# The first group's up products computed whole, and plain small operands written out directly, in a one-core encoder layer

## The chip, the cores and the metric

The kernel runs on one core of one Trainium2 chip. The metric is the device time of one execution in microseconds (us), as the median of several. The profile shows one execution, taken by the hardware profiler, with its own time.

The core's engines each have a queue of their own: TensorE (PE; its weight loads are listed as PEld), VectorE (DVE), ScalarE (ACT), GpSimd (POOL) and SyncE (SP), which here only issues DMA transfers. In the profile, "SPq" and "ACTq" are the DMA issues of SP's and ACT's instruction streams.

## What is computed

One encoder layer over 1280 tokens (256 and 1024), width 1024, in float32, and a final norm:

```python
def swiglu(h, w_gate, w_up, w_down):
    return (jax.nn.silu(h @ w_gate) * (h @ w_up)) @ w_down

for l in range(DEPTH):                      # DEPTH = 1, D_MODEL = 1024, D_FF = 2816
    x = x + 0.5 * swiglu(rmsnorm(x, norm_ffn1[l]), w_ffn1_gate[l], w_ffn1_up[l], w_ffn1_down[l])
    x = x + hybrid_mixer(rmsnorm(x, norm_mix[l]), w_in[l], ...)
    x = x + 0.5 * swiglu(rmsnorm(x, norm_ffn2[l]), w_ffn2_gate[l], w_ffn2_up[l], w_ffn2_down[l])
return rmsnorm(x, norm_final)
```

The change lies in the gate and up products of the two feed-forward blocks, called FFN1 (f = 0) and FFN2 (f = 1) here. `hybrid_mixer` (attention and gated linear attention) is not touched, but for the counts of some semaphores that it shares.

## The kernel before

Every float32 product is made in three passes with a high and a low part of each operand (`w_hi`, `w_lo`; hi x hi, hi x lo, lo x hi). The tokens are split in two halves of 640 (`HTOK`, five pairs of 128-token tiles), the 1024 inputs in two halves of 512, and the 2816 columns of a weight go in 11 groups of 256, two halves of 128. So a group of gate or up is a product of 2 x 2 blocks, and it is made by one level of Strassen's method in Winograd's form: seven products, GP1 to GP7, whose moving operand (640 columns) is a plain or combined block of the normed activations and whose stationary operand is a plain or combined block of the weight. The index q counts gate and up groups alternately, 0 to 21: q even is gate, q odd is up, and the two share the group number i = q // 2.

**Turns.** A product is made in two turns, c = 0 and 1, since 640 columns don't fit one PSUM bank. A turn has 384 or 256 columns and 12 matmuls; from q = 1 on the 256-column turn is "wide": 4 matmuls of 512 columns (two passes at once) alternate with 4 of 256. Which turn is wide depends on f. The table `GORDER` lists all turns in PE's order. The step number s counts products; `GORDER` begins with the c = 0 turns of the first `G_FIRST` = 4 steps, since the last token pair (columns of c = 1) is normed last.

**The second level.** The product GP2 (A12 times B21, B21 being activations) enters only output block C11. So the GP2 of gate and that of up of one group are joined and made by a second level: seven inner products of 320 columns (L1 in two turns, LA, LB, LB, LC, LC), each 6 matmuls, placed among the turns of the up entry (q odd). Their moving operands are seven "pieces" of B21: three plain quarters (m = 0, 1, 6) and four sums T1 to T4 (m = 2 to 5), each as high and low part, 640 KB. Group 0 uses a piece while it is made in one of two SBUF buffers; ACT's queue stores each piece into the DRAM tensor `inner_mid` (`L1630`, seven stores of 640 KB per FFN), and the groups from 1 on load them back through SP's queue into three buffers `in_b` (`L971`). For the inner weight sums, ACT keeps A12 of gate in `in_a` (`L1581`).

**Who does what around the first group.** `norm_blocks` (ACT from `L1537`, DVE from `L2092`) cuts a turned token pair from PSUM into the plain operands (GP1, GP3, B21) and the sums t1 to t4; B21 is kept in float32 only (`hs_f`). PE turns a pair with `norm_turn` (matmuls against `ident`, `L2791`), and begins the next pair only when DVE has done the low parts of an earlier one (`N["lo"]`, 6 per pair). Per weight block, ACT casts the high part (`L1574`) and DVE makes the low part (`L2132`) and the sums (`L2207` to `L2217`), five steps ahead of PE (`G_RING`). DVE adds each product from PSUM to the sums `first_p`, `first_u` (P1, U2, U3; `second_p`, `second_u` in FFN2) at `L2257`; ACT copies GP1 out of its bank (`L1592`), takes silu of finished gate blocks (`L1605`); POOL multiplies finished up blocks in. Products share PSUM banks, two for each kind of turn: GP1 (and GP2, where it is whole) uses the Z banks, GP6, GP7 and GP4 the X banks, GP5 and GP3 the Y banks. PE may write a Z bank again only when ACT's copy of GP1 is done (`kept`). Each engine runs its instructions in program order, and a DMA issue stands in the stream of the engine that issues it.

Of the kernel before, what the change touches and what calls it, by code (L numbers as in the profile page):

```python
# [30 lines left out]
P = 128  # L31
# [64 lines left out]
NP = 7  # L96
# [7 lines left out]
GU_FIRST = (GP1, GP6, GP5, GP7, GP4, GP3)  # L104
# [21 lines left out]
G_OUT = (GP7, GP4, GP3)  # L126
G_PAIRS = 2 * GROUPS
G_ENTRIES = [(q, j) for q in range(G_PAIRS) for j in (GU_UP if q % 2 else GU_GATE if q else GU_FIRST)]
# [6 lines left out]
def entry(q, j):  # L135
# [26 lines left out]
PIECE_AT = {(0, GP5, 1): 0, (0, GP7, 1): 1}  # L162
PIECE_AT.update(((1, *e), m + 2) for m, e in enumerate(INNER[:N_INNER - 2]))
PIECE_SUMS_AT = {(0, GP5, 1): 1, (0, GP4, 1): 2, (1, GP6, 1): 3, (1, GP5, 1): 4}


def a12_kept(s):

    q, j = G_ENTRIES[s]
    return q % 2 == 0 and j == (GP6 if q else GP3)  # L170


def inner_marks():

    act, dve, pool = [], [], [("b_lo", 0), ("b_lo", 1)]
    for s, c in GORDER:
        q, j = G_ENTRIES[s]
        i = q // 2
        if j == GP1 and q == 0:
            act += [("cg", 0, c)]  # L180
        if j == GP7 and c == 1 and q and q % 2 == 0:
            act += [("cg", i, 1)]
# [79 lines left out]
def build(nc, x_prompt, x_sample, norm_ffn1, w_ffn1_gate, w_ffn1_up, w_ffn1_down, norm_mix, w_in, attn_sink,  # L262
# [4 lines left out]
    with ctx:  # L267
# [60 lines left out]
        second = inner_places(1, 17920, 165888, (77312, 159744, 164864), 171520, 82432)  # L328
# [19 lines left out]
        first = inner_places(0, 161792, 133120, (122880, 128000, 133120), 138240, 140800)  # L348
# [388 lines left out]
        def cg_kept(f, i, c):  # L737
            return inner_act(f, "cg", i, 1 if i else c)
# [2564 lines left out]
```

## Time and profile before

| | |
|---|---|
| device time, median of three executions | 2182.32 us (2181.51 to 2184.72) |
| the profiled execution, its own time | 2181.47 us |
| span of its trace | 2179.3 us |
| PE busy | 2133.5 us, 98% of the span |
| DVE busy | 1613.6 us, 74% |
| ACT busy | 878.8 us, 40% |
| POOL busy | 381.5 us, 18% |
| DMA, mean over the span | 185 GB/s |

The trace covers 2179.3 us of the execution's 2181.47 us; the other 2.17 us lie around it. A row of the timeline gives the start, the duration, the engine, the source line, the operation, what is written and read, and the shape; behind it, in brackets, how long the engine had been idle and what released it. Matmuls overlap, so what one costs is the distance from its start to the next one's. "x2" at the end means two instructions in one row.

### The profile page before, as it was taken

To read this page: it belongs to the slowest core of one execution; us is meant where nothing else is said; L and a number is where in the kernel's file an instruction comes from. 1 tells how busy PE (TensorE), PEld (TensorE's weight loads), DVE (VectorE), ACT (ScalarE), POOL (GpSimd) and SP (SyncE) were. 2 spreads that over 40 slices of the span, in tenths; PEclk is the share of its full clock that TensorE was granted. 3 is DMA by queue.
4 is the path that set the end of the run, shared out by engine and by line. 5 is a ranking of instruction groups with operands and counts; after the bars stand their busy time and mean duration, and the time that the engine had idled before them with its cause. 6 is when DMAs were issued, how large, how long until landed. Compare 5 with 4: busy or idle time off the path is not lost.

```text
span 2179.3 us, 33661 instructions
## 1 busy us (share of the span) xinstructions
PE 2133.5 (98%) x11992; PEld 1919.0 (88%) x11992; DVE 1613.6 (74%) x2928; ACT 878.8 (40%) x1731; POOL 381.5 (18%) x363
## 2 busy tenths in 40 slices
PE   6899999999999999999999999899999999999998
PEld 5899999999988888888888888789999999988887
DVE  7877887888666686988754556778888788857676
ACT  7333333332343355855553334433333333343343
POOL 7311111211100002201012335321211111200000
PEclk9999999999999999999999999999999999999999
DMA  3555566556696566433255972255565556687554
GB/s 127 202 185 166 178 195 202 195 189 196 221 304 210 174 206 167 129 105 102 87 150 171 302 226 95 96 199 194 190 198 183 166 181 200 214 290 255 176 189 165
DMA packets 268168, 402.15 MB, mean 185 GB/s; under 512 B 26658, under 2 KB 162210, under 8 KB 268004
## 3 DMA queue, kind: packets, MB, share of 16 engines
q1 hardware_dynamic: 257348, 377.72, 53.9%
q10 hardware_dynamic: 10656, 22.29, 2.7%
q8 instruction: 97, 1.59, 0.3%
q14 instruction: 67, 0.55, 0.1%
HBM read 298.04 MB, written 97.65 MB: 182 GB/s over the span
## 4 chain that ended last, share of the span: by engine, by line
PE 92%; DVE 4%; issue 1%; ACT 1%; DMA 1%; SPq 0%; ACTq 0%; POOL 0%; POOLq 0%; DVEq 0%
PE ps L2863 14%; PE ps L2859 10%; PE ps L2861 8%; PE ps L2862 8%; PE ps L2871 8%; PE ps L2872 8%; PE ps L2873 8%; PE ps L2760 3%; PE ps L2762 3%; PE ps L2761 3%; PE ps L2815 2%; PE ps L2817 2%; PE ps L2816 2%; PE ps L2778 2%; PE ps L2780 2%; PE ps L2779 2%
## 5 line engine op out<-in xcount | busy, mean ns | idle before, releaser
L2871 PE MATMUL ps<-w_hi,dh 128*128 128x512 f32 x770 | 300.2, 390 | 0.0
L2873 PE MATMUL ps<-w_hi,dh 128*128 128x512 f32 x770 | 299.7, 389 | 0.0
L2863 PE MATMUL ps<-hs,w_lo 128*128 128x384 f32 (+1 forms) x848 | 261.7, 309 | 0.0
L2305 DVE TENSOR_TENSOR dh<-dr,dh 128x640 fp32r<-128x640 f32 x154 | 128.7, 835 | 158.9 <-ACT dh L1651 158.7
L2872 PE MATMUL ps<-w_lo,dh 128*128 128x512 f32 x620 | 241.2, 389 | 0.0
L1651 ACT CAST dh<-dr 128x640 fp32r<-128x640 f32 x154 | 111.9, 727 | 260.6 <-PE ps L2873 234.0
L1574 ACT CAST w_hi<-w_raw 128x512 fp32r<-128x512 f32 x154 | 95.1, 620 | 259.1 <-PE ps L2817 181.9
L2861 PE MATMUL ps<-hs,w_hi 128*128 128x384 f32 (+1 forms) x552 | 185.0, 335 | 2.8 <-DVE hs L2097 2.8
L2862 PE MATMUL ps<-hs,w_hi 128*128 128x384 f32 (+1 forms) x552 | 185.0, 335 | 0.0
L2859 PE MATMUL ps<-hs_first,w_hi 128*128 128x512 f32 x504 | 182.7, 396 | 0.0
L2859 PE MATMUL ps<-hs,w_hi 128*128 128x512 f32 x504 | 180.2, 391 | 0.0
L2862 PE MATMUL ps<-hq,w_hi 128*128 128x384 f32 x528 | 177.3, 336 | 0.0
L2873 PEld LDWEIGHTS ps<-w_hi,dh 128*128 128x128 f32 x770 | 144.5, 188 | 30.3
L2871 PEld LDWEIGHTS ps<-w_hi,dh 128*128 128x128 f32 x770 | 144.6, 188 | 30.0
L2863 PEld LDWEIGHTS ps<-hs,w_lo 128*128 128x128 f32 x848 | 160.2, 189 | 0.0
L2760 PE MATMUL ps<-h_hi,w_hi 128*128 128x512 f32 (+1 forms) x432 | 156.9, 363 | 0.0
L2762 PE MATMUL ps<-h_hi,w_lo 128*128 128x512 f32 (+1 forms) x432 | 153.3, 355 | 0.0
L2761 PE MATMUL ps<-h_lo,w_hi 128*128 128x512 f32 (+1 forms) x432 | 153.2, 355 | 0.0
L2861 PE MATMUL ps<-hq,w_hi 128*128 128x384 f32 x440 | 148.3, 337 | 4.6 <-DVE second_u L2257 3.5
L2872 PEld LDWEIGHTS ps<-w_lo,dh 128*128 128x128 f32 x620 | 116.4, 188 | 23.8
L2132 DVE TENSOR_TENSOR w_lo<-w_sum,w_hi 128x512 fp32r<-128x512 f32 x106 | 84.7, 799 | 67.8 <-ACT w_hi L1574 67.6
L1574 ACT CAST w_hi<-w_sum 128x512 fp32r<-128x512 f32 x132 | 81.1, 615 | 131.9 <-DVE w_sum L2217 74.3
(363 smaller groups left out, 5372.3 us busy)
## 6 DMA issues: line engine op xcount, KB each, us to landing
in_b<-inner_mid SPq DMA_DIRECT2D x140, 640.0 KB, 5.2
dr<-hid_mid SPq DMA_DIRECT2D x154, 320.0 KB, 3.5
w_raw<-in_w_ffn_down SPq DMA_DIRECT2D x176, 256.0 KB, 3.8
hid_mid<-st SPq DMA_DIRECT2D x88, 320.0 KB, 5.1
w_raw<-in_w_ffn_gate SPq DMA_DIRECT2D x44, 512.0 KB, 5.2
w_raw<-in_w_ffn_up SPq DMA_DIRECT2D x44, 512.0 KB, 5.0
hid_mid<-sg SPq DMA_DIRECT2D x66, 320.0 KB, 3.8
inner_mid<-piece ACTq DMA_DIRECT2D x14, 640.0 KB, 4.1
```

The costliest lines, as they stand in the source:

```text
L1574: nc.scalar.copy(g_block(s)[0][:, 0:k, :], src).then_inc(B["hi"], 1)
L2305: v.tensor_tensor(a_lo, DR[f][n % D_HID][:, :], a_hi.bitcast(F32), ALU.subtract).then_inc(W["a_lo"], 1)
L2760: mm(out, hi, rhs_hi, start=first, stop=False)
L2761: mm(out, hi, rhs_lo, start=False, stop=False)
L2762: return mm(out, lo, rhs_hi, start=False, stop=last)
L2859: mm(ps[:, G_BANKS[j][c], :], hi[:, k, :], h_both(f, j, c, k), start=begins, stop=False, skip_group_check=True)
L2861: mm(out, hi[:, k, :], b_hi, start=begins, stop=False, skip_group_check=True)
L2862: mm(out, hi[:, k, :], b_lo, start=False, stop=False, skip_group_check=True)
L2863: last = mm(out, lo[:, k, :], b_hi, start=False, stop=k == 3, skip_group_check=True)
L2871: mm(out, hi, w_h, start=first and p in D_FRESH, stop=False, skip_group_check=True)
L2872: mm(out, hi, w_l, start=False, stop=False, skip_group_check=True)
L2873: return mm(out, lo, w_h, start=False, stop=last, skip_group_check=True)
```

## The change

- **The first group is made whole** (`WHOLE = 2`): q = 0 and 1 use the seven products of one level, GP2 among them, and no inner product. The inner products begin with group 1 (q = 3). For GP2 of q = 0, silu reads the PSUM bank and writes C11's place; for q = 1, DVE multiplies GP2 in (`g_mult`). In these two entries U3 is begun by GP7 and ended by GP5. `GORDER` now begins with the c = 0 turns of five steps.
- **`norm_blocks`** writes the high part of GP2's operand into `hs` and adds one low part per pair: 7 counts per pair where there were 6.
- **Plain pieces** (m = 0, 1, 6) are now quarters of that operand, high and low part. `whole_stores` writes them from `hs` (FFN1) or `hs_first` and `hq` (FFN2) to `inner_mid`, from ACT's queue, after turn (q = 0, GP4, c = 1): 12 DMAs of 128x5x64 float32 in FFN1, 12 of 128x2x64 and 12 of 128x3x64 in FFN2; a contiguous run on the SBUF side is 64 elements, 256 bytes.
- **The sums** T1 and T3 are made by DVE with three operations each (one part each in FFN1, two in FFN2), T2 and T4 by POOL from T1 and T2 with two each; each has one ACT cast, one POOL low part and one store of 640 KB on ACT's queue.
- **Gone**: the two ACT copies of GP1 into C11's place for q = 0, the inner products, inner weight blocks and DVE additions of group 0. The load of up's second weight half no longer waits for ACT's copy of A12 in the first group, and the sums over the first group's hidden blocks move to turns of q = 2 and wait for the store of T3.

The core of the diff:

```diff
-GU_FIRST = (GP1, GP6, GP5, GP7, GP4, GP3)
+GU_FIRST = (GP1, GP6, GP2, GP7, GP5, GP4, GP3)
-G_ENTRIES = [(q, j) for q in range(G_PAIRS) for j in (GU_UP if q % 2 else GU_GATE if q else GU_FIRST)]
+G_ENTRIES = [(q, j) for q in range(G_PAIRS) for j in (GU_FIRST if q < WHOLE else GU_UP if q % 2 else GU_GATE)]
-GORDER = ([(s, 0) for s in range(G_FIRST)] + [(s, 1) for s in range(G_FIRST)]
+GORDER = ([(s, 0) for s in range(G_LEAD)] + [(s, 1) for s in range(G_LEAD)]
...
+PIECE_AT = {(0, GP3, 1): T1, (1, GP6, 0): T2, (1, GP7, 1): T4, (1, GP3, 0): T3}
+STORES_AT = {(1, GP6, 1): T1, (1, GP5, 0): T2, (1, GP5, 1): T4, (2, GP1, 0): T3}
+WHOLE_STORES_AT = (0, GP4, 1)
...
             def norm_blocks(f, i):
-                    act.wait_ge(N["lo"], 6 * i)
+                    act.wait_ge(N["lo"], 7 * i)
-                nc.scalar.copy(b21_piece(f, pair), ps[:, b + 1, :]).then_inc(N["hi"], 1)
+                nc.scalar.copy(h_piece(f, GP2, 0, pair), ps[:, b + 1, :]).then_inc(N["hi"], 1)
...
                     nc.scalar.copy(P1[f][:, lo:hi], ps[:, Z_BANKS[c], 0:n]).then_inc(S["kept"], 1)
-                    if q == 0:
-                        nc.scalar.copy(hid(f, 0)[:, lo:hi], ps[:, Z_BANKS[c], 0:n]).then_inc(L["act"], 1)
...
+            def whole_stores(f):
+                act.wait_ge(NFF[f]["lo"], 7 * HT)
+                for m, k, half in ((0, 0, 0), (1, 1, 0), (6, 1, 1)):
+                    to = inner_mid[f, m].rearrange("p (e k t n) -> p e k t n", e=2, k=2, t=HT)
+                    for a, b in B21_PARTS[f]:
+                        for e in range(2):
+                            for x in range(2):
+                                act.dma_start(to[:, e, x, a:b, :], b21(f, e, k, half, a, b)[:, x, :, :]
+                                             ).then_inc(b21_stored, 16)
...
                 if 1 in parts:
                     dve.wait_ge(N["hi"], 8 * i + 4)
+                    lo(GP2, b + 1)
                     t_free(3)
...
+            def g_mult(f, s, c):
+                if j == GP2 and q:
+                    v.tensor_tensor(to, to, by, ALU.mult).then_inc(L["dve"], 1)
...
+                if j == GP2:
+                    pe.wait_ge(*bank_kept(f, q, c))
```

Where it moves instructions, at three places. First ACT's stream from the end of q = 0's silu (`sg`) on. Before:

```order
L1605 ACTIVATE sg<-first_p 128x384 [waits gateup_added]
L1605 ACTIVATE sg<-first_p 128x256 [waits gateup_added]
L1574 CAST w_hi<-w_sum 128x512 [waits block_summed,gateup_done]
L1630 DMA inner_mid<-piece_0 128x1280 [waits pool_marks]
L1605 ACTIVATE sg<-first_u 128x384 [waits gateup_added]
L1605 ACTIVATE sg<-first_u 128x256 [waits gateup_added]
L1574 CAST w_hi<-in_a 128x256 [waits inner_dve,gateup_done]
L1630 DMA inner_mid<-piece_1 128x1280 [waits pool_marks]
L1592 COPY first_p<-ps 128x384 [waits gateup_silu,gateup_done]
L1592 COPY first_p<-ps 128x256 [waits gateup_silu,gateup_done]
```

The same place of the changed kernel:

```order
L1656 ACTIVATE sg<-first_p 128x384 [waits gateup_added]
L1656 ACTIVATE sg<-first_p 128x256 [waits gateup_added]
L1616 CAST w_hi<-w_raw 128x512 [waits block_summed,gateup_done]
L1679 DMA inner_mid<-hs 128x5x64 [waits norm_ffn1_lo]
L1679 DMA inner_mid<-hs 128x5x64 x11
L1656 ACTIVATE sg<-first_u 128x384 [waits gateup_added]
L1656 ACTIVATE sg<-first_u 128x256 [waits gateup_added]
L1616 CAST w_hi<-w_sum 128x512 [waits block_summed,gateup_done]
L1665 CAST piece_0<-piece_sum_0 128x640 [waits inner_dve]
L1637 COPY first_p<-ps 128x384 [waits gateup_silu,gateup_done]
L1637 COPY first_p<-ps 128x256 [waits gateup_silu,gateup_done]
```

Two stores of pieces have given way to twelve in a row, ahead of the copies (`COPY first_p<-ps`) of GP1 of q = 1. In FFN2, 24 stand there.

Second, PE's stream in q = 1, where the first turn behind GP1's wide turn stood. Before, an inner product, bound to its piece:

```order
L2859 MATMUL ps<-hs,w_hi 128x512 [waits inner_act,gateup_kept,block_lo]
L2863 MATMUL ps<-hs,w_lo 128x256
...
L2815 MATMUL ps<-piece_0,w_hi 128x320 [waits pool_marks,block_lo]
L2816 MATMUL ps<-piece_0,w_hi 128x320
L2817 MATMUL ps<-piece_0,w_lo 128x320
```

In the changed kernel, the end of GP6's wide turn and the two turns of GP2 of q = 1:

```order
L2936 MATMUL ps<-hs,w_hi 128x512
L2940 MATMUL ps<-hs,w_lo 128x256
L2938 MATMUL ps<-hs,w_hi 128x384 [waits gateup_kept,block_lo]
L2939 MATMUL ps<-hs,w_hi 128x384
L2940 MATMUL ps<-hs,w_hi 128x384
...
L2936 MATMUL ps<-hs,w_hi 128x512 [waits gateup_wide,block_lo]
L2940 MATMUL ps<-hs,w_hi 128x256
```

The turn that follows GP6 is now GP2, and it waits for `gateup_kept`, ACT's copy of GP1 of the same q.

Third, DVE's stream in FFN1's norm of the third pair. Before:

```order
L2110 TENSOR_TENSOR first_t<-first_t,ps 128x512 [waits norm_ffn1_hi,norm_ffn1_t_lo]
L2097 TENSOR_TENSOR hs<-ps,hs 128x512
L2115 TENSOR_TENSOR first_t<-ps,first_t 128x512 [waits norm_ffn1_lo,norm_ffn1_hi,norm_ffn1_t_lo]
L2120 TENSOR_TENSOR first_t<-ps,first_t 128x512 [waits norm_ffn1_lo,norm_ffn1_t_lo,norm_ffn1_hi]
L2123 TENSOR_TENSOR first_t<-ps,first_t 128x512 [waits norm_ffn1_t_lo]
L2097 TENSOR_TENSOR hs<-ps,hs 128x512
```

The changed kernel:

```order
L2157 TENSOR_TENSOR first_t<-first_t,ps 128x512 [waits norm_ffn1_hi,norm_ffn1_t_lo]
L2144 TENSOR_TENSOR hs<-ps,hs 128x512
L2162 TENSOR_TENSOR first_t<-ps,first_t 128x512 [waits norm_ffn1_lo,norm_ffn1_hi,norm_ffn1_t_lo]
L2144 TENSOR_TENSOR hs<-ps,hs 128x512 [waits norm_ffn1_hi]
L2168 TENSOR_TENSOR first_t<-ps,first_t 128x512 [waits norm_ffn1_lo,norm_ffn1_t_lo]
L2171 TENSOR_TENSOR first_t<-ps,first_t 128x512 [waits norm_ffn1_t_lo]
L2144 TENSOR_TENSOR hs<-ps,hs 128x512
```

One more low part (GP2's) has come between the sums.

## Rows read from the trace of the kernel before

**Rows 1.** Timeline of PE in FFN1: the prologue's wait, two stalls, q = 2's first matmul.

```profile
43.04 1.09 PE L2791 MATMUL ps<-ident,hs_f 128*128 128x128 f32 x8 [1.50 <-DVE first_t L2120]
...
72.75 0.61 PE L2815 MATMUL ps<-piece,w_hi 128*128 128x320 f32 x1 [2.61 <-DVE up_c L2187]
...
92.80 0.38 PE L2815 MATMUL ps<-piece,w_hi 128*128 128x320 f32 x1 [3.16 <-issue]
...
98.77 0.34 PE L2861 MATMUL ps<-hs,w_hi 128*128 128x384 f32 x1
```

**Rows 2.** Timeline of PE in FFN2: four stalls, and q = 2's first matmul.

```profile
1387.90 0.66 PE L2861 MATMUL ps<-hq,w_hi 128*128 128x384 f32 x1 [3.49 <-DVE second_u L2257]
...
1404.71 0.38 PE L2815 MATMUL ps<-piece,w_hi 128*128 128x320 f32 x1 [0.52 <-DVE up_c L2187]
...
1411.33 0.39 PE L2815 MATMUL ps<-piece,w_hi 128*128 128x320 f32 x1 [1.14 <-POOL piece L1398]
...
1424.82 0.60 PE L2815 MATMUL ps<-piece,w_hi 128*128 128x320 f32 x1 [3.64 <-issue]
...
1430.61 0.39 PE L2859 MATMUL ps<-hs_first,w_hi 128*128 128x512 f32 x1
```

**Rows 3.** Windows: stretch, length, busy (count) per engine, PEclk, DMA share, GB/s.

```profile
72.70:76.10 3.40, 3.35 (x12) 3.38 (x13) 3.07 (x7) 0.62 (x1) 0.00 (x0) 0.50 0.00 0
...
93.00:96.50 3.50, 3.50 (x14) 3.50 (x14) 2.56 (x4) 1.36 (x2) 3.24 (x3) 0.53 0.78 259
...
1387.90:1393.60 5.70, 5.70 (x21) 5.70 (x22) 2.19 (x4) 2.95 (x7) 2.08 (x2) 0.50 0.01 3
...
1424.80:1427.80 3.00, 2.98 (x10) 2.81 (x11) 1.72 (x4) 1.35 (x2) 2.40 (x3) 0.50 0.62 203
```

**Rows 4.** Timeline of PE: the spacing of matmuls of 320, 512+256 and 384 columns.

```profile
89.18 0.31 PE L2816 MATMUL ps<-piece,w_hi 128*128 128x320 f32 x1
89.33 0.31 PE L2817 MATMUL ps<-piece,w_hi 128*128 128x320 f32 x1
...
98.31 0.28 PE L2863 MATMUL ps<-hs,w_lo 128*128 128x256 f32 x1
...
98.66 0.28 PE L2863 MATMUL ps<-hs,w_lo 128*128 128x256 f32 x1
...
98.95 0.33 PE L2862 MATMUL ps<-hs,w_hi 128*128 128x384 f32 x1
```

**Rows 5.** Timeline of ACT (ACTq: DMA issues in its stream) at FFN1's first piece store.

```profile
62.55 0.53 ACT L1605 ACTIVATE sg<-first_p 128x384 f32<-128x384 f32 x1 [1.20 <-DVE first_p L2257]
62.97 0.34 ACTq L1630 DMA_DIRECT2D inner_mid<-piece  x1
62.98 0.40 ACT L1605 ACTIVATE sg<-first_p 128x256 f32<-128x256 f32 x1
63.28 0.60 ACT L1574 CAST w_hi<-w_sum 128x512 fp32r<-128x512 f32 x1
...
66.89 0.74 ACT L1592 COPY first_p<-ps 128x384 f32<-128x384 f32 x2
68.32 0.62 ACT L1574 CAST w_hi<-in_a 128x512 fp32r<-128x512 f32 x1 [0.70 <-DVE in_a L2146]
68.85 0.72 ACT L1622 CAST piece<-piece_sum 128x640 fp32r<-128x640 f32 x1
```

**Rows 6.** Timeline of SP's DMA issues: loads of `hq` in a row, one weight load.

```profile
1241.49 8.20 SPq L1198 DMA_DIRECT2D hq<-o_mid  x8
...
1266.69 10.13 SPq L1270 DMA_DIRECT2D hq<-o_mid  x20
...
1381.08 0.58 SPq L867 DMA_DIRECT2D w_raw<-in_w_ffn_gate  x1
```

**Rows 7.** Timeline of DVE: an operation beside POOL, and FFN2's wait for weights.

```profile
28.96 1.77 DVE L2213 TENSOR_TENSOR w_raw<-w_raw 128x512 f32<-128x512 f32 x1
...
1384.46 0.69 DVE L2207 TENSOR_TENSOR w_sum<-w_raw 128x512 f32<-128x512 f32 x1 [2.21 <-DMA w_raw<-in_w_ffn_up]
```

More of the change, by code:

```diff
@@ L125, with u3_first, u3_last, outputs @@
 G_ADDS = (GP6, GP5, GP7, GP4, GP3)
-G_OUT = (GP7, GP4, GP3)
+WHOLE = 2
 G_PAIRS = 2 * GROUPS
-G_ENTRIES = [(q, j) for q in range(G_PAIRS) for j in (GU_UP if q % 2 else GU_GATE if q else GU_FIRST)]
+def u3_first(q):
+    return GP7 if q < WHOLE else GP5
+def u3_last(q):
+    return GP5 if q < WHOLE else GP7
+def outputs(q):
+    return (GP2, GP5, GP4, GP3) if q < WHOLE else (GP7, GP4, GP3)
+G_ENTRIES = [(q, j) for q in range(G_PAIRS) for j in (GU_FIRST if q < WHOLE else GU_UP if q % 2 else GU_GATE)]
 G_STEPS = len(G_ENTRIES)
@@ L189, in inner_marks @@
             pool += [("mult", i)]
-        for n in [5] if s == 1 and c else G_AFTER[(s, c)] if s >= G_LEAD - 1 else []:
+        if q == 1 and j == GP2:
+            dve += [("mult", 0, c)]
+        for n in G_AFTER[(s, c)]:
             at, kind_of = G_ENTRIES[n]
-            if kind_of == GP3 and at % 2 == 0:
+            if first_difference(n):
                 dve += [("summed", at // 2, 1)]
@@ L1413, in gate_up @@
             def gate_up(f):
-                for m in range(2):
-                    piece_lo(f, m)
+                piece_sum(f, T2)
+                piece_lo(f, T1)
+                piece_sum(f, T4)
+                piece_lo(f, T2)
+                piece_lo(f, T4)
                 for s, c in GORDER:
@@ L1556, in g_hi @@
                 q, j = G_ENTRIES[s]
-                raws = [g_raw(f, q, e) for e in range(2)]
                 if s >= G_RING:
@@ L1576, in keep_a12 @@
             def keep_a12(f, i):
-                if i:
+                if i > 1:
                     act.wait_ge(*lo_made(f, 2 * i - 1, LC))
+                else:
+                    for read in b21_read(f):
+                        act.wait_ge(*read)
                 act.wait_ge(*g_loaded(f, 2 * i, 0))
@@ L1600, in g_evict @@
                     nc.scalar.copy(hid(f, 0), P1[f][:, :]).then_inc(L["act"], 1)
-                if j in G_OUT and q % 2 == 0:
-                    act.wait_ge(*added(f, s, c))
-                    src = {GP7: U3, GP4: P1, GP3: U2}[j][f][:, lo:hi]
-                    out = hid(f, {GP4: 1, GP3: 2, GP7: 3}[j])[:, lo:hi]
+                if j in outputs(q) and q % 2 == 0:
+                    if j == GP2:
+                        act.wait_ge(*done(f, s, c))
+                        src = ps[:, Z_BANKS[c], 0:n]
+                    else:
+                        act.wait_ge(*added(f, s, c))
+                        src = {u3_last(q): U3, GP4: P1, GP3: U2}[j][f][:, lo:hi]
+                    out = hid(f, {GP2: 0, GP4: 1, GP3: 2, u3_last(q): 3}[j])[:, lo:hi]
                     nc.scalar.activation(out, src, ACT.Silu).then_inc(S["silu"], 1)
@@ L2209, in g_sums @@
                     v.tensor_tensor(s2, s1, a11, ALU.subtract).then_inc(B["summed"], 1)
-                if j == GP6 and (q or f == 0):
+                if j == (GP2 if q < WHOLE else GP6) and (q or f == 0):
                     dve.wait_ge(*lo_made(f, q, GP1))
@@ L2233, in g_evict @@
                 of, rest = ps[:, G_BANKS[j][c], 0:n], ps[:, G_BANKS[j][c], 512 - n:512]
-                if two and j == GP1:
-                    to = p1[:, part]
+                if two and j in (GP1, GP2):
+                    to = (p1 if j == GP1 else u3)[:, part]
                     dve.wait_ge(*kept(f, s, c))
@@ L2736, in _ @@
             norm_blocks(1, HT - 1)
-            for s in range(2, G_FIRST):
+            for s in range(2, G_LEAD):
                 g_evict(1, s, 0)
@@ L2827, in g_step @@
                 if q == 0:
-                    name, n, count = {GP1: (NFF[f]["lo"], 6, 2), GP6: (t_low[f], 4, 2), GP7: (t_low[f], 4, 4),
-                                      GP5: (t_low[f], 4, 1), GP4: (t_low[f], 4, 3), GP3: (NFF[f]["lo"], 6, 6)}[j]
+                    name, n, count = {GP1: (NFF[f]["lo"], 7, 2), GP6: (t_low[f], 4, 2), GP2: (NFF[f]["lo"], 7, 4),
+                                      GP7: (t_low[f], 4, 4), GP5: (t_low[f], 4, 1), GP4: (t_low[f], 4, 3),
+                                      GP3: (NFF[f]["lo"], 7, 7)}[j]
                     if f and c and n == 4:
```

349 lines of the change are left out of this document (191 added, 158 removed).

## The prediction

> **What bounds the kernel now.** I read the share of busy time first: PE works 98% of the span, so a change can only take PE's work, its few waits, or the slow clock behind a wait. Then the waits of PE, and in the timeline where they lie. Around the first group of FFN1 PE stands still twice, 2.61 us before an inner product that waits for a DVE addition, and 3.16 us before the last one but one; the trace names nothing for the latter ("issue"), and in the program it waits for a piece that goes through ACT and POOL [rows 1]. In FFN2 there are four, of 3.49, 0.52, 1.14 and 3.64 us [rows 2]. Then the windows: behind four of these stalls the granted clock is 0.50 to 0.53, that is 1.2 GHz in place of 2.4, for 3.4, 3.5, 5.7 and 3.0 us [rows 3]. Half of each stretch is lost: 1.7, 1.7, 2.85 and 1.5 us. I count up to the start of q = 2, at 98.77 and 1430.61 [rows 1, 2], and take the rest of the kernel as unchanged: from there on both have the same products, and the reloaded pieces are first needed in q = 3, some 20 us later.
>
> **PE's work.** Matmuls of 384 columns are 0.17 to 0.18 us apart (98.77 to 98.95), a pair of 512 and 256 columns 0.35 (98.31 to 98.66), those of 320 columns 0.145 (89.18 to 89.33) [rows 1, 4]. So a turn of 384 columns takes 2.09, one of 256 1.40, a whole product 3.5, an inner one 0.87. Each FFN adds two products (7.0) and drops seven inner ones (6.1): **+0.9 us** each.
>
> **Stalls that go.** All six stood at inner products of group 0 or behind piece work on DVE. FFN1: 2.61 + 3.16 + 1.7 + 1.7 = **-9.2**. FFN2: 3.49 + 0.52 + 1.14 + 3.64 + 2.85 + 1.5 = **-13.1**.
>
> **The norm.** The extra low part (0.6 us of DVE per pair, by the step from one DVE row to the next, 0.69 long) delays the turning of the next pair. In FFN1 it lies on the path twice, in the first product's start and in the fourth turning, about 1.4 with the waits. But PE now does GP2's c = 0 turn before the last pair is turned, where it idled 1.50 [rows 1]; that wait goes: **-0.1** in sum. FFN2 has more cover, **-0.3**. The bounds: at best the whole 1.5 is won, at worst all five low parts lie on the path, 3.0 per FFN.
>
> **A wait that stays in FFN2.** GP4's c = 1 turn needs U3's addition, which DVE does behind its wait for up's weights (2.21 idle at 1384.46 [rows 7]). PE comes 3.2 later (GP2, less 0.3); the load is issued some 1.2 later, behind one more low part (0.6), and the two piece sums ahead of the addition (0.8) are gone: 3.49 - 3.2 + 1.2 + 0.6 - 0.8 = **+1.3**. Between 0 and the old 3.49.
>
> **The stores on ACT's queue.** This is the new thing and decides. They stand ahead of silu (two), a weight cast, a piece cast and the copy that frees GP1's bank; PE's turn of GP2 of q = 1 waits for that copy. What an issue costs, from the nearest rows: one alone 0.34, and ACT's computing runs on beside it (62.97 against 62.98, with the next operation on time) [rows 5]; so they start when the cast ahead starts, but a row of them is a chain of issues. Twenty `hq` loads of 256 runs took 10.13, 0.51 each; eight others 8.20, 1.03 each, while earlier transfers were pending; a weight load of 1024 runs behind another 0.58 [rows 6], 0.62 with the gap. I take 0.51 for FFN2's (256 and 384 runs), 0.56 for FFN1's (640 runs, between). DMA is idle at that time (share 0.00 at 72.7, 0.01 at 1387.9 [rows 3]), which is why I stay near the unburdened row.
>
> FFN1: silu of GP4's first turn, at 62.55 before [rows 5], comes one product less 0.1 later, 66.0; the cast 0.7 later at 66.7. Twelve issues: 6.7, until 73.4. Then silu 0.43 and 0.30, cast 0.53, piece cast 0.72, copy 0.37 [rows 5], 2.3 in all: 75.7. PE without stalls would begin q = 2 at 98.77 - 9.2 + 0.9 - 0.1 = 90.4, and GP2 of q = 1 five products (17.4) earlier, at 73.0. So it stands for 2.7 us, and the clock falls as it did after 2.61 (1.7). Net: -8.4 + 2.7 + 1.7 = **-4.0**.
>
> FFN2: GP4's second turn is ready at 1387.90 - 3.49 + 3.2 = 1387.6, starts at 1388.9, ends 1391.0; addition, silu, and the cast starts at 1392.2. 24 issues: 12.2, until 1404.4. The same five operations, the copy of 256 columns for 384, 2.2, and since the first turn is the wide one here, a DVE addition of 0.4: 1407.0. PE without this stall: 1430.61 - 13.1 + 0.9 - 0.3 + 1.3 = 1419.4, GP2 at 1402.0. So 5.0 of standing and, between the 1.5 and the 2.85 of before, 2.2 for the clock. Net: -11.2 + 7.2 = **-4.0**.
>
> The other new work has cover: the sums on POOL (four passes of 640 columns, then low parts) and the stores of T1 to T4 are due in q = 3, PE's 20 us. The two ACT copies that go are no path.
>
> A page bears on this. The Trainium skill, "DMA: Bandwidth & Descriptors", Specifications, gives 512 bytes as the least run at line rate and says that below it the engine reads, modifies and writes. The runs here are 256 bytes in SBUF. The rows show loads of 512-byte runs only, so no row here bears it out; by it the third case below would be the likely one.
>
> **Sum.** 2181.47 - 4.0 - 4.0 = **2173.5 us** for an execution like the profiled one, which lies 0.9 below the median of 2182.32. 0.1 us per issue is 3.6 us in all. Break-even (2181.47) is at 0.22 us more per issue, some 0.75.
>
> **Rivals.**
> 1. Cheaper stores. If an issue in a row costs as one alone, 0.38 with the gap, FFN1 gains 12 x 0.18 = 2.2 and FFN2 24 x 0.13 = 3.1: 2168.2. If ACT isn't held at all, the full 8.4 + 11.2 come: 2161.9. For it: the store beside ACT's work at 62.97 [rows 5]. Against: each `hq` issue is paced at 0.51 with SP doing nothing else [rows 6].
> 2. Nothing gained: DVE late. One DVE operation of 512 columns beside POOL took 1.77 in place of 0.69 [rows 7]. About eight of DVE's operations stand between the landing of up's weights and the cast ahead of the stores, and POOL now has four additions more there. If four of the eight in each FFN are stretched by 1.1, the stores begin 4.4 later and both gains are eaten: 2173.5 + 8.8 = 2182.3. The Trainium skill, "SBUF — State Buffer", section "SBUF: two separate sides", says of the port pair that DVE and GpSimd share that a GpSimd operation and a DVE one with two SBUF inputs exclude each other for a whole instruction; by that rule the stretch is one POOL operation long. Against it: POOL's sums begin only after T1, that is after GP3's additions, and at 62 to 70 POOL has little else.
> 3. Slower: the stores back up. At 1.03 each, as the eight `hq` loads [rows 6], FFN1 loses 12 x 0.47 = 5.6 and FFN2 24 x 0.52 = 12.5: 2191.6. It is slower by 0.2% from about 0.9 per issue. For it: short runs, twelve and 24 transfers with nothing between; against it: idle DMA engines.
>
> **How the numbers follow.** 0.2% (4.4 us) is what a measurement can tell from no change. Forecast 0.43 (2170 to 2178, of it 0.03 above 2177.1); rival 1 0.17; rival 2 0.22 (2178 to 2187, of it 0.02 beyond 2185.9); rival 3 0.18. Faster 0.40 + 0.17 = 0.57; same 0.03 + 0.20 = 0.23; slower 0.02 + 0.18 = 0.20. The range leaves out the lower half of rival 1 and the upper half of rival 3: 2165 to 2189.
>
> **What would show it.** In ACT's stream, a row of 12 issues of some 6.7 us from about 67 on, and one of 24 of some 12 us from 1392; right behind, two silus and two casts, the copy, and PE's wait at the first matmul of GP2 of q = 1, of about 2.7 and 5 us, with a half-clock stretch behind each. q = 2 starts near 94.8 and 1422.6 (1426.6 less FFN1's 4.0). No wait at an inner product of q = 3. The forecast is wrong if ACT computes on during the row, if an issue takes 0.9 or more, if the cast ahead of the row starts later than 69, or if PE waits elsewhere, above all in the norm for low parts beyond 1.5 us.

## The result: slower by 0.67%, and the profile after

The changed kernel takes 2196.77 us (median of four, 2196.49 to 2197.64), the kernel before 2182.46 us (2181.51 to 2184.72): a ratio of 1.0067, with a 95% interval of 1.0054 to 1.0079. The forecast was a gain of 8 us, to 2173.5; what came is a loss of 14.3, outside the range. The profiled execution of the changed kernel took 2196.83 us, with a span of 2195.0 beside 2179.3 before.

Its page, first the span and PE's row of section 1 (busy us, share, instructions), then the first rows of the chain that ended last:

```profile
span 2195.0 us, 33664 instructions
...
PE 2133.8 (97%) x11996; PEld 1918.8 (87%) x11996; DVE 1616.3 (74%) x2922; ACT 869.7 (40%) x1716; POOL 383.4 (17%) x364
...
PE 89%; DVE 4%; DMA 2%; issue 2%; ACT 1%; ACTq 1%; SPq 1%; POOL 0%; DVEq 0%; POOLq 0%
```

PE has nearly the same work (busy for 2133.8 us beside 2133.5, four matmuls more), so the loss is waiting and the slow clock behind a wait. The waits of PE, us in total, times, longest:

```profile
PE ps L2936 <- DVE second_u L2318: 9.2, 3, 8.5
...
PE ps L2938 <- DVE first_u L2318: 8.0, 2, 7.4
PE ps L2936 <- DVE second_p L2296: 7.7, 1, 7.7
PE ps L2938 <- ACT first_p L1637: 6.3, 2, 6.1
```

Of the six stalls of [rows 1, 2] five are gone, and of the 3.49 us one 1.00 is left (at 1394.77). Four larger ones have come, two per FFN. PE's timeline shows where:

```profile
77.35 0.66 PE L2938 MATMUL ps<-hs,w_hi 128*128 128x384 f32 x1 [6.12 <-ACT first_p L1637]
...
96.83 0.34 PE L2938 MATMUL ps<-hs,w_hi 128*128 128x384 f32 x1
...
118.28 0.66 PE L2938 MATMUL ps<-hs,w_hi 128*128 128x384 f32 x1 [7.42 <-DVE first_u L2318]
...
1415.28 0.77 PE L2936 MATMUL ps<-hs_first,w_hi 128*128 128x512 f32 x1 [7.71 <-DVE second_p L2296]
...
1434.63 0.39 PE L2936 MATMUL ps<-hs_first,w_hi 128*128 128x512 f32 x1
...
1457.15 0.76 PE L2936 MATMUL ps<-hs_first,w_hi 128*128 128x512 f32 x1 [8.49 <-DVE second_u L2318]
```

The stalls at 77.35 and 1415.28 stand before GP2 of q = 1, where the forecast put them. Those at 118.28 and 1457.15 stand at GP3 of q = 2, the last gate product but one of group 1, and no case of the forecast had them. Behind each the clock is at its lower level for some 4 us, as in [rows 3] (columns as there; 0.54 to 0.56 is a mean, with some tenths of a us at the upper level):

```profile
77.30:81.90 4.60, 4.55 (x15) 4.54 (x16) 3.48 (x7) 1.84 (x4) 1.16 (x1) 0.55 0.55 175
118.20:122.90 4.70, 4.62 (x15) 4.58 (x16) 4.63 (x9) 1.16 (x2) 0.00 (x0) 0.55 0.55 210
```

**The account by stage.** q = 2 of FFN1 starts at 96.83 in place of 98.77: 1.9 gained. FFN2's first product starts 7.0 later than before (1369.18 and 1362.14): 9.0 lost in between, 7.42 of standing and some 2 of clock. FFN2's q = 2 starts at 1434.63 in place of 1430.61, 4.0 later: 3.0 gained in FFN2's first group. The end is 15.7 later: 11.7 lost behind it, 8.49 and 2 of clock among them. So both first groups are faster, 4.9 in all, and 20.7 are lost behind them. Nearly all of that is lost at once: the 120 matmuls from q = 2's first on take 20.8 us in the trace before, and 30.4 (FFN1) and 31.1 (FFN2) now, which is 19.9 of the 20.7.

**The first kind of stall: the row of stores.** ACT's timeline in FFN1 (as [rows 5]) and the end of the row in FFN2:

```profile
66.10 8.72 ACTq L1679 DMA_DIRECT2D inner_mid<-hs  x11
74.87 0.83 ACT L1656 ACTIVATE sg<-first_u 128x384 f32<-128x384 f32 x2 [8.27 <-issue]
...
76.74 0.74 ACT L1637 COPY first_p<-ps 128x384 f32<-128x384 f32 x2
...
1412.44 0.83 ACT L1656 ACTIVATE sg<-second_u 128x256 f32<-128x256 f32 x2 [12.12 <-issue]
```

ACT stands for 8.27 and 12.12 us behind the issues. One issue takes 0.80 us in FFN1 (8.72 and a gap over 11; the first, at 65.68, took 0.42) and 0.54 in FFN2 (24 from 1399.38 to 1412.40). Then two silus, two casts and the copy, in the order forecast; PE's turn of GP2 begins with the copy's end, in FFN2 with DVE's addition behind the copy. Ahead of FFN1's row, from 60.5 to 66.0, the DMA share is 0.00; during the row the stores, with one load of weights (512 KB) beside them, keep the DMA engines busy all the time, at only 231 GB/s (columns as above, the last two DMA share and GB/s):

```profile
66.10:74.80 8.70, 5.13 (x30) 4.53 (x28) 4.48 (x7) 0.50 (x1) 3.06 (x2) 0.99 1.00 231
```

In FFN2's row the share is 0.77, at 177 GB/s.

**The second kind: a late weight load.** DVE's timeline before the stall at 118.28, and SP's issues:

```profile
115.51 0.69 DVE L2266 TENSOR_TENSOR w_sum<-w_raw 128x512 f32<-128x512 f32 x1 [7.60 <-DMA w_raw<-in_w_ffn_up]
```

```profile
100.75 1.34 SPq L999 DMA_DIRECT2D in_b<-inner_mid  x3
102.14 1.96 SPq L893 DMA_DIRECT2D hid_mid<-sg  x3
104.22 0.41 SPq L890 DMA_DIRECT2D w_raw<-in_w_ffn_up  x1
```

The kernel before, SP's issues at the same place of the program:

```profile
92.72 1.30 SPq L971 DMA_DIRECT2D in_b<-inner_mid  x3
94.07 7.32 SPq L870 DMA_DIRECT2D hid_mid<-sg  x3
101.50 0.45 SPq L867 DMA_DIRECT2D w_raw<-in_w_ffn_up  x1
```

Before, three pieces (3 x 640 KB) were issued 6 us ahead of q = 2's start and 8.8 us ahead of the weights. Now they are issued 4 us behind q = 2's start, and the weights 3.5 us behind them. They wait for DVE's last addition of T3, since the buffers `in_b` lie on the memory that T3 is made from; it ran from 99.79 to 100.6. The stores of hidden blocks stand behind the pieces in SP's stream and are held with them. So 2.9 MB (pieces and hidden blocks) stand ahead of the 512 KB of weights on this queue, and the load lands 11.3 us after its issue, where the same load took 5.0 before (the views of DMA issues, before and after):

```profile
w_raw<-in_w_ffn_up SPq DMA_DIRECT2D x1, 512.0 KB, 5.0
...
w_raw<-in_w_ffn_up SPq DMA_DIRECT2D x1, 512.0 KB, 11.3
```

The windows show the DMA engines busy all the time and, in the second, PE idle:

```profile
104.00:110.00 6.00, 6.00 (x36) 5.75 (x35) 3.77 (x8) 1.52 (x3) 1.69 (x2) 1.00 1.00 333
110.00:115.50 5.50, 0.86 (x6) 0.50 (x4) 0.00 (x0) 0.00 (x0) 0.00 (x0) 1.00 1.09 358
```

DVE has the addition for PE's bank (`first_u`, at 117.58) behind the two sums of those weights and one of hidden blocks, and PE stands for that.

### The profile page after: what moved, and what is told of

It is laid out like the page before. It is cut to its first block, busy times and chain, and to the rows that moved or that the text cites. A ratio compares the mean times of both kernels' runs of the same rounds, so it can differ in the third digit from the quotient of the medians.

```text
span 2195.0 us, 33664 instructions
## 1 busy us (share of the span) xinstructions
PE 2133.8 (97%) x11996; PEld 1918.8 (87%) x11996; DVE 1616.3 (74%) x2922; ACT 869.7 (40%) x1716; POOL 383.4 (17%) x364
## 4 chain that ended last, share of the span: by engine, by line
PE 89%; DVE 4%; DMA 2%; issue 2%; ACT 1%; ACTq 1%; SPq 1%; POOL 0%; DVEq 0%; POOLq 0%
PE ps L2940 12%; PE ps L2936 10%; PE ps L2950 8%; PE ps L2949 8%; PE ps L2948 8%; PE ps L2938 7%; PE ps L2939 7%; PE ps L2837 4%; PE ps L2838 4%; PE ps L2839 4%; DMA w_raw<-in_w_ffn_up 2%; PE ps L2888 2%; PE ps L2890 2%; PE ps L2889 2%; PE ps L2855 2%
## 5 line engine op out<-in xcount | busy, mean ns | idle before, releaser
L2940 PE MATMUL ps<-hs,w_lo 128*128 128x384 f32 (+1 forms) x864 | 266.6, 309 | 0.0
L2938 PE MATMUL ps<-hs,w_hi 128*128 128x384 f32 (+1 forms) x564 | 189.7, 336 | 16.4 <-DVE first_u L2318 8.0
L2939 PE MATMUL ps<-hs,w_hi 128*128 128x384 f32 (+1 forms) x564 | 189.2, 335 | 0.0
L2939 PE MATMUL ps<-hq,w_hi 128*128 128x384 f32 x536 | 179.7, 335 | 0.0
L2938 PE MATMUL ps<-hq,w_hi 128*128 128x384 f32 x448 | 150.7, 336 | 2.0 <-POOL hq L1377 1.0
```

The lines of the kernel that those rows point to most:

```text
L2938: mm(out, hi[:, k, :], b_hi, start=begins, stop=False, skip_group_check=True)
L2939: mm(out, hi[:, k, :], b_lo, start=False, stop=False, skip_group_check=True)
L2940: last = mm(out, lo[:, k, :], b_hi, start=False, stop=k == 3, skip_group_check=True)
```

## Experiments

Two theories stand behind this reading. A: the row of issues holds ACT. B: the pieces, released late, put their bytes ahead of a weight load. The kernel before was timed beside each set again (medians 2180.95, 2181.55 and 2180.80 us), so ratios are the measure; the changed kernel's is 1.0067. All edits but e4's act in both FFNs.

**e1: the plain stores on SP's queue.**

```diff
-                if at == WHOLE_STORES_AT:
-                    whole_stores(f)
...
                     if q + 1 < G_PAIRS:
                         load_gu(f, 2 * q + 2)
+                    if q == 1:
+                        whole_stores(f)          # now with sp in place of act
```

> The changed kernel, with the plain stores issued from SP's queue, behind the load of the next gate weights, instead of ACT's. Theory A (the row of issues holds ACT, and PE waits for the copy of GP1 behind it): PE's waits of 6.12 us at 77.35 and 7.71 us at 1415.28 go, with half of the 6.83 us of half clock behind each: 6.1 + 7.7 + 3.4 + 3.4 = 20.6 less, so 2196.8 - 20.6 = about 2176; the waits of 7.42 and 8.49 us in q = 2 stay, perhaps somewhat longer since PE comes earlier (up to the whole 20: then 2185 to 2196). Rival (the copy is late for another reason, such as DVE's sums or the DMA traffic itself): the waits stay, 2195 to 2198.

Measured 2182.92 us (10 runs), ratio 1.0006 (0.9997 to 1.0016): 13.3 us less than the changed kernel, where 20.6 were expected. SP's issue row and PE's waits:

```profile
57.78 9.67 SPq L1009 DMA_DIRECT2D inner_mid<-hs  x12
...
74.63 0.41 PE L2938 MATMUL ps<-hs,w_hi 128*128 128x384 f32 x1 [2.06 <-ACT first_p L1649]
...
115.36 0.66 PE L2938 MATMUL ps<-hs,w_hi 128*128 128x384 f32 x1 [8.25 <-DVE first_u L2318]
```

Theory A holds: in FFN2 the wait of 7.71 is gone, in FFN1 2.06 of 6.12 are left. Those hang on another thing, DVE's three additions of T1, which stand ahead of GP3's second addition; ACT's silu waits for that, the copy stands behind silu. The wait in q = 2 grew from 7.42 to 8.25 in FFN1, since PE comes 3.7 us earlier and the stall ends only 2.9 earlier; in FFN2 it fell from 8.49 to 8.17. The row costs SP 0.81 us per issue, so a row is not dear because ACT issues it; but two loads of weights (1 MB) were still under way when SP's row began, so the equal price is no clean comparison of the two queues.

**e4: twelve stores as twenty-four.** In FFN1 each store is cut in 2 and 3 runs per partition, as FFN2 has them.

```diff
-        IN_B_STORES = [3 * 4, 3 * 4 * 2]
+        IN_B_STORES = [3 * 4 * 2, 3 * 4 * 2]
...
-                    for a, b in B21_PARTS[f]:
+                    for a, b in B21_PARTS[1]:
```

> The changed kernel, with FFN1's twelve plain stores of 5 runs per partition row split into 24 of 2 and 3 runs, as FFN2 has them; the same bytes and runs. In FFN1 an issue took 0.80 us (11 in 8.72), in FFN2 0.51 to 0.57. Theory R (the number of runs sets the pace, above a floor of 0.51 to 0.57 per issue): 24 issues take the larger of 12 x 0.80 = 9.6 and 24 x 0.55 = 13.2, so 13.2, and PE's wait at 77.35 grows by 3.6 to about 9.7; the time rises by 3.6, to 2200.4. Rival (0.80 is what a transfer costs at this place, whatever its size, because the DMA engines are shared): 24 x 0.80 = 19.2, the wait about 15.7, 2206.

Measured 2201.49 us (one run). ACT's row and PE's wait:

```profile
66.16 12.62 ACTq L1679 DMA_DIRECT2D inner_mid<-hs  x23
...
81.30 0.66 PE L2938 MATMUL ps<-hs,w_hi 128*128 128x384 f32 x1 [10.02 <-ACT first_p L1637]
```

0.55 per issue, and the wait grew by 3.9 (3.6 expected), so it is not the place alone that makes an issue cost 0.80. The windows of DMA hint at what does. In the row of twelve the engines are busy all the time (1.00 at 231 GB/s, above); in the row of 24, with the same bytes, they are not:

```profile
66.20:78.80 12.60, 5.08 (x30) 4.47 (x28) 4.48 (x7) 0.45 (x1) 3.07 (x2) 0.80 0.79 183
```

I read this so: the smaller stores (256 and 384 runs) go at the pace of issuing, about 0.55 each, and the larger ones (640 runs) at the pace of the DMA engines, 0.80 each. The bytes of a store and its number of runs changed together, so which of the two counts is not shown.

**e8: the row three turns later.**

```diff
-WHOLE_STORES_AT = (0, GP4, 1)
+WHOLE_STORES_AT = (1, GP1, 1)
```

> The changed kernel with the row of plain stores three turns later in ACT's stream, behind the copies of GP1 of q = 1. Theory A (what hurts is what stands behind the row on ACT): the wait before GP2 of q = 1 (6.12 at 77.35, 7.71 at 1415.28) goes, since the copies are ahead of the row now; the row ends near 80, and the casts of weights behind it, for GP5 and GP4 of q = 1, are needed from about 79: a wait of 0 to 5 at one of them. 2180 to 2190. Rival (the transfers themselves disturb): no change, 2195 to 2198.

Measured 2199.45 us (one run), more than both cases had (2180 to 2190, and 2195 to 2198):

```profile
74.64 0.41 PE L2938 MATMUL ps<-hs,w_hi 128*128 128x384 f32 x1 [2.06 <-ACT first_p L1637]
88.20 0.41 PE L2938 MATMUL ps<-hs,w_hi 128*128 128x384 f32 x1 [1.32 <-DVE first_u L2318]
...
1428.41 0.76 PE L2936 MATMUL ps<-hs_first,w_hi 128*128 128x512 f32 x1 [8.31 <-DVE second_u L2318]
```

The wait before GP2 shrank as in e1, and others came behind the row, in FFN2 one of 8.31 us, more than what went: there DVE stands for 10.21 us until ACT, behind the row, has cast a weight (1421.67), and PE for DVE. What hurts is whatever stands behind the row on ACT; neither of the two places tried has 9 or 13 us to spare.

**e2: the weight load ahead of pieces and hidden blocks.** It needed a wait of silu for the three stores of hidden blocks.

```diff
-                    load_gu(f, 2 * q + 1)
+                    if q != 3:
+                        load_gu(f, 2 * q + 1)
...
+                    if q == 2:
+                        load_gu(f, 7)
                     if q % 2 == 0:
                         for m in range(3):
                             load_in_b(f, i + 1, m)
                         store_hidden(f, i)
```

> The changed kernel, with one load of up's weights (first used by DVE at 115.5) issued from SP ahead of the three loads of pieces (640 KB each) and the three stores of hidden blocks, in both FFNs; a wait on those stores is added on ACT. Theory B (2.9 MB are issued just before that load, since SP stood for the sum T3 until 100.75, and the load lands 11.3 us after its issue): the waits of 7.42 and 8.49 us go with their half clock, 7.4 + 8.5 + 3.4 + 3.4 = 22.7 less, about 2174. Rival (DVE or the weight's buffer is late, not the transfer): no change within 2 us, 2195 to 2198.

Measured 2186.95 us (10 runs), ratio 1.0027 (1.0017 to 1.0037): 8.7 less, not 22.7. The two waits of 7.42 and 8.49 are gone wholly, as B says. In their place:

```profile
127.92 0.38 PE L2893 MATMUL ps<-in_b,w_hi 128*128 128x320 f32 x1 [2.15 <-DVE up_c L2251]
...
1462.60 0.38 PE L2893 MATMUL ps<-in_b,w_hi 128*128 128x320 f32 x1 [1.92 <-DVE up_c L2251]
```

Behind each of these the clock is at its lower level again for some 3.3 us (a mean of 0.56 from 129.4 to 132.7 and from 1464.0 to 1467.3), and FFN2 has one more wait, of 1.30 us. That is a good part of the 14 us that are missing.

**e5: the weight load ahead of the hidden blocks alone** (0.96 MB), with the same wait of silu; the load of e2 stands between `load_in_b` and `store_hidden`.

> The changed kernel with the load of up's weights ahead of the three stores of hidden blocks (0.96 MB) alone, behind the three loads of pieces (1.92 MB). By theory B the landing moves earlier by the share of what stood ahead: 0.96 of 2.9 MB at about 340 GB/s is 2.8 us, so the waits of 7.42 and 8.49 fall by about 2.8 each, the time to about 2191; e2, with all 2.9 MB behind, took them away wholly. Rival (the wait hangs on the issue time alone): no change, 2196.

Measured 2191.09 us (one run), as expected. PE's waits:

```profile
116.88 0.41 PE L2943 MATMUL ps<-hs,w_hi 128*128 128x384 f32 x1 [4.33 <-DVE first_u L2323]
...
1452.09 0.58 PE L2941 MATMUL ps<-hs_first,w_hi 128*128 128x512 f32 x1 [4.59 <-DVE second_u L2323]
```

The wait fell by 3.1 us in FFN1 and by 3.9 (8.49 to 4.59) in FFN2, 2.8 expected from the bytes at about 340 GB/s. With e2 this is a dose and its response: nothing moved, 0.96 MB moved and 2.9 MB moved leave a wait of 7.4, 4.3 and 0 us in FFN1.

**e3: e1 and e2 together.**

> Both edits. If A and B are the whole story, 20.6 + 22.7 = 43.3 come off: about 2153.5, 1.3% under the kernel before. If another wait stands next behind either, 2160 to 2175.

Measured 2171.96 us (4 runs), ratio 0.9954 (0.9939 to 0.9969), faster than the kernel before: 24.6 less than the changed kernel, about the sum of e1 and e2 (22.0), and not the 43.3 expected. Other waits stand next: 2.06 before GP2, and in the second group 1.16 and 2.17 (FFN1), 1.30 and 1.95 (FFN2). ACT's timeline names the source of the second group's:

```profile
111.46 0.53 ACT L1673 ACTIVATE sg<-first_u 128x384 f32<-128x384 f32 x1 [8.34 <-DMA hid_mid<-sg]
```

That is the wait which this order needs: now the hidden blocks leave late.

**e6: T3's additions earlier, stores on SP's queue.**

```diff
-DVE_SUMS_AT = {(0, GP3, 0): T1, (1, GP4, 1): T3}
+DVE_SUMS_AT = {(0, GP3, 0): T1, (1, GP5, 1): T3}
```

> The changed kernel, with the plain stores on SP's queue (as e1) and DVE's three additions of T3 made two products earlier, behind (q = 1, GP5, c = 1); SP's order of loads stays that of the change. Theory B says that the load of up's weights is late since T3 holds the piece loads, and 2.9 MB are issued just before it. With T3's sum some 5 us earlier, those loads are issued near 92 in place of 98 to 101, and the load of weights comes near 101 with most of them landed: the wait of 8.25 (e1) falls to 0 to 3 us in FFN1, likewise in FFN2, and the time from 2182.9 to about 2182.9 - 2 x 6 - 2 x 3 to 5 of half clock = 2162 to 2165. Rival: the load needs its own conditions (ACT's copy of A12, a low part on DVE) and comes no earlier, the wait stays over 6, 2178 to 2184.

Measured 2176.85 us (10 runs), ratio 0.9979 (0.9969 to 0.9988): 5.9 less than e1, a third of what I expected. SP's issues and DVE's wait:

```profile
92.71 1.34 SPq L999 DMA_DIRECT2D in_b<-inner_mid  x3
94.09 1.69 SPq L893 DMA_DIRECT2D hid_mid<-sg  x3
97.21 0.39 SPq L890 DMA_DIRECT2D w_raw<-in_w_ffn_up  x1
...
106.90 0.69 DVE L2266 TENSOR_TENSOR w_sum<-w_raw 128x512 f32<-128x512 f32 x1 [4.71 <-DMA w_raw<-in_w_ffn_up]
```

The pieces come 4.7 us earlier than in e1 (97.41 there), which shows that T3 held them. But the load of weights has come 3.6 earlier too (100.85 there) and DVE takes it up only 9.7 us after its issue. What counts is the distance from the pieces' issue to the load's: it is 4.5 us here, and was 8.8 before.

**e9: stores on SP's queue, pieces behind both weight loads.**

```diff
+                    if q == 3:
+                        for m in range(3):
+                            load_in_b(f, 1, m)
                     if q % 2 and q >= 3:
                         store_sums(f, i)
                     if q % 2 == 0:
-                        for m in range(3):
-                            load_in_b(f, i + 1, m)
+                        if q > 2:
+                            for m in range(3):
+                                load_in_b(f, i + 1, m)
                         store_hidden(f, i)
```

> Plain stores on SP's queue (as e1), and the first three loads of pieces issued behind the two loads of up's and gate's weights of q = 3, not ahead of the stores of hidden blocks; nothing else changes, T3's sum stays where the change has it. By theory B the 1.92 MB no longer stand before the weights: the waits of 8.25 and 8.17 us of e1 go, and the half clock behind them (10.2 us in each, 5.1 lost): 2182.9 - 16.4 - 10.2 = 2156 for e9, 2156 to 2162 with small waits left. The pieces are issued near 101 and must be there at about 117. Rival (DVE or ACT work in q = 2 and 3 is too dense, as e3's 1.2, 2.2, 1.3 and 2.0 us of waits hint): like e3, 2168 to 2173.

Measured 2166.91 us (2165.51 to 2168.66, 4 runs), ratio 0.9938 (0.9921 to 0.9955): 0.6% faster than the kernel before, the lowest median of all. The stores of hidden blocks no longer stand behind the pieces, so they leave early as well, at 91.33. SP's issues, and what is left of PE's waits:

```profile
98.16 0.38 SPq L890 DMA_DIRECT2D w_raw<-in_w_ffn_up  x1
100.78 0.38 SPq L890 DMA_DIRECT2D w_raw<-in_w_ffn_gate  x1
101.35 1.91 SPq L999 DMA_DIRECT2D in_b<-inner_mid  x3
```

```profile
73.33 0.41 PE L2942 MATMUL ps<-hs,w_hi 128*128 128x384 f32 x1 [2.06 <-ACT first_p L1653]
...
90.77 0.34 PE L2942 MATMUL ps<-hs,w_hi 128*128 128x384 f32 x1
...
122.61 0.38 PE L2892 MATMUL ps<-in_b,w_hi 128*128 128x320 f32 x1 [1.36 <-DVE up_c L2250]
...
1414.84 0.39 PE L2940 MATMUL ps<-hs_first,w_hi 128*128 128x512 f32 x1
```

No stall over 2.1 us is left in either gate/up part behind the norm, and no stretch at the lower clock follows one. What remains against the expected 2156 is a number of waits of 1 to 2 us, mostly on DVE, and a clock loss that I had put too high: I had taken half of the whole stretch of 6.8 or 10.2 us, while part of each lies in the stall itself.

**e11: the late pieces alone, stores on ACT.**

> The changed kernel with the late piece loads of e9 alone; the plain stores stay on ACT's queue. By theory B the waits of 7.42 and 8.49 go with their half clock (3.4 each): 2196.8 - 22.7 = 2174; the waits of 6.1 and 7.7 before GP2 stay. Rival as for e9: 2185, as e2.

Measured 2181.14 us (10 runs), ratio 1.0001 (0.9992 to 1.0011): 14.4 less than the changed kernel. 6.11 and 7.74 stay before GP2, 7.42 has become 1.81, 8.49 is gone. So of the 28.1 us between the changed kernel and e9 (1.0067 and 0.9938 of some 2181), the order of loads and stores on SP's queue is worth 14.4 (e11) and the place of the stores 13.7 (e9 against e11) or 13.3 (e1): they add up.

**e7 and e10: T1's additions behind GP3's second addition** (`DVE_SUMS_AT` and `PIECE_AT` for T1 at (0, GP3, 1) and (1, GP1, 1)), on top of e6 and of e9.

> As e6, and T1's three additions on DVE moved behind the addition of GP3's second turn, its cast on ACT behind the copies of GP1 of q = 1. In e3, ACT's copy at 71.93 still came 2.06 late, behind silu of GP3's second turn, which waited for T1's additions on DVE (67.57 to 70.02). Expected: that wait of 2.06 goes, with the half clock behind it in FFN1 (1.7), FFN2 gains little: 2 to 4 below e6, about 2159 to 2162, 1% under the kernel before. Rival: T2's and T4's sums on POOL come 2.5 later, and with them the piece loads: no gain against e6.

> e9 with T1's additions on DVE behind the second addition of GP3 and T1's cast on ACT behind the copies of GP1, as e7. In e7 the wait of 2.06 before GP2 of q = 1 fell to 0.68, but the pieces came later and others grew. With the pieces off the critical order: 1 to 3 us below e9. Rival (T2 and T4 late on POOL slow DVE in q = 1, as in e7): 1 to 4 above e9.

Measured 2180.65 (ratio 0.9994, 0.9985 to 1.0003) against e6's 2176.85, and 2168.69 (0.9948, 0.9933 to 0.9963) against e9's 2166.91. The wait of 2.06 fell to 0.69 in e10, and 0.60 at 86.77 and 1.67 at 1426.58 came. The rival was right for e7, which is 3.3 us slower than e6: the pieces were issued 1.3 us later (94.05 beside 92.71), as was POOL's second sum of T4 (84.01 beside 82.62), and the wait for the weights in FFN1 grew from 4.46 to 5.99. For e10 the difference is within the intervals. So a later T1 gained nothing; in e7 because T2 and T4 hang on it, and in e10 that was not looked into.

## Why the prediction was wrong, point by point

**What it left out: the queue behind a wait.** The failed step is the clause on the pieces in the first part ("the reloaded pieces are first needed in q = 3, some 20 us later") and its repetition under "The other new work has cover". It asked when the pieces are needed, and never what stands behind their loads on SP's queue. There stand the hidden blocks and up's weights, which landed 5.0 us after their issue before and 11.3 now; and T3's sum is a new wait of these loads. The term "from there on both have the same products", put at 0, measured +20.7 us. Of these the order on SP's queue alone gives back 14.4 (e11), and e2 and e5 show the mechanism. In e9 some 8 us are still lost there (8.0 gained at q = 2, 3.3 at FFN2's first product; 15.8 gained at FFN2's q = 2, 12.4 at the end). Waits of 0.99, 1.36 and 1.55 us (the last at an inner product in FFN2) are half of it. Counted matmul by matmul against the trace before, 3.3 us in FFN1 and 2.6 in FFN2 are lost within the first 200 matmuls from q = 2 on, the rest in small steps along the layer, 0.9 of it in the mixer, which the change doesn't touch; four executions of e9 differ by some 3 us among themselves, so that rest is not told from chance.

**The stores.** The mechanism was right: the row starts just ahead of the cast (65.68; forecast 66.7), ACT stands, the five operations follow, and PE waits for the copy with the lower clock behind. The size was off in FFN1: 0.76 per issue in the mean (0.80 behind the first) where I took 0.56, 9.1 us in place of 6.7. The term mis-sized is the interpolation between 0.51 (256 runs) and 0.62 (1024 runs [rows 6]): the latter was one load behind a single other, before a row of them had built up. In e8's row the first four issues took 0.5 to 0.6, with a DMA share of 0.57, and the next eight 0.90 each (7.17 for 8), with a share of 1.06. The reason given, that DMA is idle at that time, looked at a moment without the row: the row itself filled the engines. The eight `hq` loads at 1.03 each, which the forecast left to its third rival, stood in such a stretch in the kernel before, there with earlier loads under way:

```profile
1241.50:1249.70 8.20, 8.20 (x66) 6.70 (x65) 5.52 (x11) 3.00 (x5) 2.91 (x1) 1.00 1.07 370
```

In FFN2 an issue took 0.54 for 0.51, 13.0 us for 12.2.

But the longer row is only half of the longer wait. In FFN1 PE stood for 6.12 in place of 2.7: it could go on at 77.35, 1.6 later than forecast, and it arrived at 71.23, 1.8 earlier than the 73.0 of the forecast, because the norm gained more than thought (below). FFN2's 7.7 for 5.0 splits the same way: counted from its first product, which comes 7.0 later, PE goes on 1.3 later and arrives 1.5 earlier.

**The norm.** Forecast -0.1 in FFN1. The first product came 0.8 later (34.53), more than the 0.6 of one low part, but the product behind the last turning starts at 44.85, 0.2 earlier than before, with GP2's turn of 2.1 already done: -2.3. Of that, 1.7 is clock: before, a stretch at the lower clock lay on PE's path,

```profile
35.20:38.60 3.40, 3.40 (x15) 3.30 (x15) 3.40 (x4) 2.11 (x4) 3.40 (x4) 0.50 0.03 5
```

and in the changed kernel such a stretch lies ahead of the first product, from 17 to 30.7, and PE still waits 2.08 us for DVE behind it. I have no run that shows why it moved. In FFN2 a wait of 1.53 at 1373.08 went and the others there stayed within 0.6.

**The stalls that go, and the rest.** Five of the six went, and the sixth is the wait that the forecast kept in FFN2: GP4's second turn waited 1.00, forecast 1.3. Without the stores' stall FFN1's first group gains 10.1 by the sum (1.9 and 6.1 and 2.1 of clock), forecast 8.4, and the norm's 2.2 covers the difference. e9 shows it directly: q = 2 starts at 90.77, 8.0 earlier than before, with 2.06 us of waiting still in it. In FFN2 it starts at 1414.84, 15.8 earlier, 12.5 of them in FFN2 (3.3 at its first product); forecast 11.2. PE's busy time rose by 0.3 us, where the forecast had 1.8 more work in all.

**The rivals.** The third (stores backing up, 2191.6) had the right sign and part of the right cause: in FFN1 0.80 is halfway from 0.56 to its 1.03, and the engines were full. But by itself that would have left the time at about 2177: forecast sum 2173.5, and 3 us more for issues. The second (DVE stretched beside POOL) does happen, an operation took 2.05 us at 85.46, beside one of POOL of 1.56 at 85.40; but it would have begun FFN1's row late, and that began 1.0 earlier than forecast, with no stretched operation of DVE in the 5 us ahead of it. The Trainium skill, "DMA: Bandwidth & Descriptors", Specifications, by which a transfer needs 512 bytes for line rate and is read, modified and written below that, made a backing up the likelier case. The runs bear out that short runs are slow: with these 256-byte runs the engines were busy all the time at 231 GB/s, with the loads of q = 2 at 333. That they read and modify is not visible here, and whether the size of a run or a cost per run makes the difference is not told apart, since every plain store had runs of 256 bytes.

## What to carry to other kernels

When a change adds a wait to a DMA issue, list what stands behind it on that queue and when each of those is needed, not only when the waiting transfer is; a load that is issued late may lose more to the bytes now bunched ahead of it than to its own lateness. A row of DMA issues holds the engine whose queue carries it (8 and 12 us here for 2 MB in 256-byte runs), so put it on an engine that computes nothing at that time. Both were repaired without touching the change's idea, and e9, with the stores on SP and the pieces behind the weights, turned +0.67% into -0.62%.

## What the runs showed of the hardware

- In a row of stores in 256-byte runs, an issue took about 0.55 us with 256 and 384 runs per store, with the DMA share at 0.79 and 183 GB/s (e4), and 0.80 with 640 runs, with the share at 1.00 and 231 GB/s. In e8 the first four issues of 640 runs took 0.5 to 0.6, the next eight, with the engines full, 0.90.
- With 2.9 MB ahead on the same queue, at 333 to 358 GB/s, 512 KB of weights landed 11.3 us after issue (5.0 before). With 2.0 MB of it moved behind, and the other 0.96 MB issued some 7 us ahead, DVE waited 2.18 us for them in e11 and not at all in e9.
- The stretch at the lower clock begins inside a long stall, not at its end. In the last 2.2 us of the stall before 77.35 the granted clock is down already,

```profile
75.10:77.30 2.20, 0.00 (x0) 0.00 (x0) 0.69 (x1) 2.20 (x6) 0.39 (x1) 0.50 0.80 180
```

and only the 4.6 us behind it lie on PE's work. That is why a stall of 6 us costs about 2 us of clock and not half of the whole stretch.
